# Neighbourhood heads computed two at a time on row and column halves of TensorE

## The chip, the cores and the metric

The kernel runs on one core of a Trainium2 chip. The metric is the device time of one execution, in microseconds. TensorE multiplies, ScalarE (ACT) and VectorE (DVE) do the rest of the arithmetic, and SyncE (SP) issues the loads from HBM.

## What is computed

Two parts follow each other in one program: a two-layer block with a mixture of experts (untouched here), and a two-layer transformer over x (256 tokens) and a context (256 tokens) of width 1024. Its first mixer has 4 differential heads and 8 neighbourhood heads of width 64. The neighbourhood heads, cut to what matters:

```python
# x's queries: keys of x inside a 16-column window of the 64-wide grid, with a bias, and all context keys
s_nb = einsum('bchd,bicjhd->bhcij', q_r, k_r) * scale + bias
s_ctx = einsum('bchd,bnhd->bhcn', q_r, kcx) * scale
p = softmax(concatenate([s_nb, s_ctx], -1))
out_x = einsum(p_nb, v_r) + einsum(p_ctx, vcx)
# the context's queries: plain attention over the context's keys, 8 heads of 64
b_c = plain_attention(heads(bq_c, 8), heads(bk_c, 8), heads(bv_c, 8))
```

The kernel takes x's neighbourhood as a dense 512-wide row of scores (256 context keys, 256 x keys) with a bias matrix of 128 x 256 per head and query block that is -1e30 outside the window.

## The kernel before

**Dense work.** A weight tile is 128x2048 f32 (1 MB). SP loads it to one of 3 RAW places, ScalarE rounds it to its high half WH, VectorE makes the low half WL (3 places of each), and TensorE forms every product as three (L1639 to L1641). With 256 columns a tile is 48 products, in four parts of 12.

**The plan.** `Plan` writes one list of units by hand-made rules and a clock of its own; every engine walks through this same list and takes its units from it. `lin` (L371) adds a weight tile to the list of tiles when its turn comes. Heads are Python generators (`Chain`). After each part of a dense block `weave` (L736) gives every live chain whose time has come one step; `lanes` says how many chains are live, in part 1 two. `yield t` in a chain means: not before t on the plan's clock.

**One head** (`head`, L565): scores `s` (two query blocks, qb 0 and 1), maximum and exponential `e`, normalising `n`, transposes `t`, and after both blocks the values `v`, then a copy of the result. Keys and queries of head hd lie on partitions 0 to 63 when hd is even and 64 to 127 when it is odd, so a score is a product over 64 rows (L1721); values give 64 columns (L1793). With a bias the score is followed by a second product that adds it (L1727). `part=0` are the context's queries, 256 keys; `part=1` those of x, 512 keys.

**Pairs** (`twins`, L639): the same for two heads, until now used by the last mixer's windowed heads (L1345). `s2` (L1732) puts both scores (L1741) and then both masks or biases (L1754 there); `v2` (L1757) takes the heads' values in turns (L1769), one in columns 0 to 63 and one in 64 to 127. It already has a branch for near heads with bias, which no caller used.

**The bias loads.** The bias of head hd lies in one of two places (slot 10 + hd % 2: BIAS and PQ). `head` adds the load when head hd-2 is scored and the chain is live:

```python
while hd > 1 and f"n1.{hd - 2}" not in self.scored:
    yield self.clock + 0.5
t = self.add_tile(("bias", hd), ..., slot=10 + hd % 2, ...)
t.end = ("s", name, 1, 0)
self.put("loads", ("bias", hd))
```

SP issues all tiles, weights and biases alike, in the order of the list (`upto`, L2980, `load`, L2968). Before a load it waits for the end of the tile that had the place before: for a weight tile its split on VectorE, for a bias the scores of qb 1 of the head that used it. `splits_ahead` (L788) keeps a tile's split on ScalarE and VectorE behind the unit for which a load before it in the list must wait.

**Around the change.** `near(0)` and `near(1)` put the context's heads between the dense stages of the mixer's projections; `p.until` ends this with four or five lanes. Then come, with two lanes, the differential heads d1.0 to d1.3 and the near heads n1.0 to n1.7 of x, woven into the context's output projection and its gated layer (`g0c`).

Of the kernel before, what the change touches and what calls it, by code (L numbers as in the profile page):

```python
# [302 lines left out]
class Plan:  # L303


    def __init__(self, io, mem, v):
        self.io = io
        self.units, self.tiles, self.tile, self.stage = [], [], {}, {}
        self.region, self.phase, self.by_split = [], 0, {}
        self.banks, self.tmp, self.pp, self.pt = Rotation(), Rotation(), Rotation(), Rotation()  # L310
        self.heads, self.norms, self.ropes = {}, {}, {}
        self.side, self.live, self.lanes, self.clock = [], [], 2, 0.0
        self.busy, self.at, self.freed_at, self.split_at, self.taken = {A: 0.0, V: 0.0}, {}, {}, {}, {}
        self.n = {"split": 0, "small": 0}
        self.bgc, self.fgc, self.ppc, self.ptc, self.tmpc, self.tmpg = BG, FG, TMP4, TMP4, TMP4, TMP4
        self.ready, self.scored = set(), set()
        self.small = {}
        self.ada = [(l, q) for l in range(2) for q in range(12)]
        self.group, self.grouped = {}, []
        self.asked, self.unturned, self.copied, self.fill_at, self.late = [], [], None, 0.0, []  # L320
        first_order(self)
        second_order(self)
        place_tiles(self.tiles, mem, v)
        place_tiles(self.other[0], mem, v)
        self.units = splits_ahead(self.units, self.tiles, self.tile)
        self.region = splits_ahead(self.region, self.other[0], self.other[1])
# [312 lines left out]
    def twins(self, a, b, nk, bias=False, late=False, **spec):  # L639

        for name, hd in ((a, spec["hd"]), (b, spec["hd"] + 1)):
            self.heads[name] = dict(spec, nk=nk, qbs=2, members=1, bias=bias, sub=False, hd=hd)
        u, near, pair = 0.43 * nk / 256, spec["kind"] == "near", (a, b)

        def room(rotation, choices):
            return sum(x not in rotation.held for x in choices) > 1

        def chain():
            if near and bias:
                hd = spec["hd"]  # L650
                while hd and f"n1.{hd - 1}" not in self.scored:
                    yield self.clock + 0.5
                for x in (hd, hd + 1):
                    t = self.add_tile(("bias", x), self.io["bias"][x], 1, 512, split=False, slot=10 + x % 2,
                                      after=() if hd else [("ps", "v", f"d0.{i}") for i in range(4)] + [("ps", "v", f"n0.{i}") for i in range(8)] + [("band_r",)])
                    t.end = ("s", f"n1.{x}", 1, 0)
                    self.put("loads", ("bias", x))
            blocks, turned = head_needs(self.heads[b])
            blocks, turned = head_needs(self.heads[a])[0] + blocks, head_needs(self.heads[a])[1] + turned
            ready = max([self.at.get(k, 0.0) for k in blocks] + [self.at.get(("roped", r), 0.0) for r in turned])  # L660
            yield ready
            copied = 0.0
            for qb in range(2):
                if qb == 0 and not late:
                    while not room(self.pt, self.ptc):
                        yield self.clock + 0.3
                    for x in pair:
                        self.pt.take(("pt", x), self.ptc, True)
                while len(self.banks.held) > 5:
                    yield self.clock + 0.3  # L670
                free = max([self.bank(("s", x, qb, 0), self.bgc, True) for x in pair])
                at = self.put("s2", a, b, qb, cost=1.25 * u + (0.25 + 0.4 * near) * 2 * bias, after=free)
                if qb:
                    self.scored.update(pair)
                yield at
                while not room(self.pp, self.ppc):
                    yield self.clock + 0.3
                exped, scaled = {}, {}
                for x in pair:
                    self.pp.take(("pp", x, qb), self.ppc, True)  # L680
                    self.small[x, qb, 0] = 4 * (self.n["small"] % 32)
                    self.n["small"] += 1
                    exped[x] = self.freed_at["s", x, qb, 0] = self.put("e", x, qb, 0, after=at)
                    self.banks.let(("s", x, qb, 0))
                yield exped[a]
                for x in pair:
                    scaled[x] = self.put("n", x, qb, 0, after=exped[x])
                yield scaled[a]
                if qb == 0 and late:
                    while not room(self.pt, self.ptc):  # L690
                        yield self.clock + 0.3
                    for x in pair:
                        self.pt.take(("pt", x), self.ptc, True)
                for x in pair:
                    free = self.bank(("t", x, qb), self.bgc)
                    copied = self.freed_at["t", x, qb] = self.put("t", x, qb, cost=u / 2, after=max(free, scaled[x]))
                    self.pp.let(("pp", x, qb))
                yield self.clock
            yield copied
            free = self.bank(("v", a), self.bgc)  # L700
            copied = self.freed_at["v", a] = self.put("v2", a, b, cost=2 * u, after=max(free, copied))
            for x in pair:
                self.pt.let(("pt", x))
                self.at["head", x] = copied
                self.ready.add(x)
        self.side.append(Chain(chain()))

    def rope(self, name, **spec):
# [474 lines left out]
def second_order(p):  # L1183
# [44 lines left out]
    wab0 = Stage("wab0", "rows", "res", io["w_out_ab"], 8, 0, D, "HP", norm="ab0", gate=(0, 0, 1))  # L1228

    def near(t):  # L1230
        for hd in range(4 * t, 4 * t + 4):
            p.head(f"n0.{hd}", 256, kind="near", part=0, hd=hd)

    def diff(t):
        for i in (2 * t, 2 * t + 1):
# [2 lines left out]
    def ropes(g, t):  # L1238
        for blk in (2 * t, 2 * t + 1):
            p.rope(f"{g.name}{blk}", buf=g.more["dst"], blk=blk, n0=T, stage=g.name)  # L1240
    p.lanes = 4
    near(0)
    for t in range(2):
        for g in (aq, ak, av):
# [5 lines left out]
    for g in (bq, bk, bv):  # L1250
        p.lin(g, 1)
        p.turn_one()
    near(1)
    p.begin(wab0, 0)
    p.begin(wab0, 1)
# [7 lines left out]
    p.ppc, p.ptc, p.tmpc = (20, 21), (20, 21), (0, 1)  # L1263
    for i in range(4):
        p.head(f"d1.{i}", 512, members=2, sub=True, kind="diff", part=1, i=i)
    for hd in range(8):
        p.head(f"n1.{hd}", 512, bias=True, kind="near", part=1, hd=hd)
    p.norm("c0.1", src="CTX", tmp="G01", gn=(0, 1, 1), dst="HP", n0=0, of="wab0")
    p.lin_all(wab0, p.follow("c0.1"))
    p.put("gains", 0, 1)  # L1270
# [90 lines left out]
    for j in range(4):  # L1361
        t = p.weight(("wc", j), wc.w, j, 2, 1024)
# [192 lines left out]
def head_needs(spec):  # L1555

    k = spec["kind"]
    if k == "mem":
        return [(f"{n}{spec['l']}", i) for n in ("kvK", "kvV", "q") for i in (6, 7)], []
    if k == "diff":  # L1560
        t = spec["i"] // 2
        need = [("aq", 2 * t), ("aq", 2 * t + 1), ("ak", 2 * t), ("ak", 2 * t + 1)] + [("av", 4 * t + i) for i in range(4)]
        return need, [f"{n}{i}" for n in ("aq", "ak") for i in range(4)] if spec["part"] else []
    if k == "near":
        t = spec["hd"] // 4
        return [("bq", 2 * t), ("bq", 2 * t + 1), ("bk", 2 * t), ("bk", 2 * t + 1)] + [("bv", 4 * t + i) for i in range(4)], []
    hd = spec["hd"]
    return [("ck", 2), ("ck", 3), ("cv", 2), ("cv", 3)], [f"cq{hd // 2}", f"ck{hd // 4}"]
# [1652 lines left out]
```

How the kernel before makes its waits and increments, by code:

```python
    def wait_ge(self, what, *key):  # L90
        what = self.pre + what
        if self.counting:
            return
        n = self.ledger.value[(what,) + key]
        if self.seen.get(what, 0) < n:
            self.eng.wait_ge(self.ledger.sem(what), n)
            self.seen[what] = n
# [5 lines left out]
    def freed(self, key):  # L103
        if key is None or self.counting:
            return
        by = self.ledger.handed.get((self.pre,) + key)
        if by is not None:
            return self.wait_for(by)
        for what in ("free_a", "free_d"):
            if (self.pre + what,) + key in self.ledger.value:
                return self.wait_ge(what, *key)
        raise KeyError(key)
# [1 line left out]
    def wait_for(self, thing):  # L115
        n = self.ledger.value[thing]
        if self.seen.get(thing[0], 0) < n:
            self.eng.wait_ge(self.ledger.sem(thing[0]), n)
            self.seen[thing[0]] = n
# [1 line left out]
    def turn(self, made):  # L121
        made.then_inc(*self.done("turn_" + self.tag, self.steps))
        self.wait_ge("turn_" + self.tag, self.steps)
        self.steps += 1
# [1469 lines left out]
    def weight(key):  # L1595
        t = plan.tile[key]
        pe.wait_ge("w_hi", t.s)
        pe.wait_ge("w_lo", t.s)
        return t
# [1 line left out]
    def consts():  # L1601
        pe.wait_ge("par")
        pe.wait_ge("cst")
# [1 line left out]
    def lin(name, t, i, part, parts, side=None):  # L1605
# [27 lines left out]
        for j, (lh, ll, rh, rl) in enumerate(pairs):  # L1633
            if norm:
                pe.wait_ge("lo", norm, ks[j] // 2)
            if "each" in g.more:
```

## Time and profile before

| | |
|---|---|
| median of 3 runs | 3349.06 us (3346.85 to 3357.35) |
| profiled execution | 3353.13 us, span 3351.3 us |
| TensorE busy | 3197.1 us, 95% |
| VectorE, ScalarE busy | 2331.1 us (70%), 1828.2 us (55%) |
| mean granted TensorE clock | 0.977 |
| HBM | 718.87 MB read, 215 GB/s over the span |

All times in the trace are microseconds from the start of the span. Ends of products on TensorE are modelled, so starts are compared with starts. A product in full f32 leaves two records, which is why one score shows as x2.

### The profile page before, as it was taken

What the parts mean: (1) busy time and instruction counts of PE and PEld (TensorE: products, weight loads), DVE (VectorE), ACT (ScalarE), POOL (GpSimd) and SP (SyncE); (2) the same over time, 40 slices, a digit from 0 to 9 for tenths busy, and PEclk for the clock granted to TensorE, in tenths of its full rate; (3) what the DMA queues carried; (4) which work ended last, traced back from release to release, by engine and by line L of the source; (5) the groups of instructions that cost most, each with busy time, mean ns of one, the idle gap of its engine ahead of it and who ended that gap; (6) DMA issues with size and microseconds to landing.
All of it is one profiled execution on the core that took longest, in us unless ns stands there. A gap on an engine that the chain in (4) does not pass through costs nothing.

```text
span 3351.3 us, 56010 instructions
## 1 busy us (share of the span) xinstructions
PE 3197.1 (95%) x24147; PEld 2976.5 (89%) x24147; DVE 2331.1 (70%) x2984; ACT 1828.2 (55%) x2180; POOL 0.2 (0%) x4
## 2 busy tenths in 40 slices
PE   8999999999999899999999999989899999998898
PEld 7998999999889799999999999878777889985798
DVE  6877655577876588888888888755575556466555
ACT  5564544455545477777777777643464445335443
POOL 0000000000000000000000000000000000000000
PEclk9999999999999899999999999999899999998899
DMA  6433565454335699899899999632223466530353
GB/s 256 167 131 134 178 237 201 152 194 172 115 133 181 239 380 357 334 359 357 336 356 358 338 354 356 249 132 75 102 95 129 157 236 239 214 144 33 151 187 116
DMA packets 102812, 723.62 MB, mean 216 GB/s; under 512 B 11424, under 2 KB 13344, under 8 KB 16672
## 3 DMA queue, kind: packets, MB, share of 16 engines
q1 hardware_dynamic: 102560, 719.97, 58.0%
q8 instruction: 194, 3.18, 0.4%
q14 instruction: 58, 0.48, 0.0%
HBM read 718.87 MB, written 1.05 MB: 215 GB/s over the span
## 4 chain that ended last, share of the span: by engine, by line
PE 78%; DVE 11%; ACT 7%; issue 2%; DMA 1%; SPq 0%; DVEq 0%; ACTq 0%
PE PS L1639 14%; PE PS L1640 14%; PE PS L1641 14%; PE PS L1590 6%; PE PS L1592 6%; PE PS L1591 6%; DVE WL L2424 4%; ACT WH L2015 3%; PE PS L1951 3%; PE PS L1952 3%; PE PS L1953 3%; PE PS L1793 1%; PE PS L1694 1%; PE PS L1721 1%; PE PS L1937 1%
## 5 line engine op out<-in xcount | busy, mean ns | idle before, releaser
L2424 DVE TENSOR_TENSOR WL<-RAW,WH 128x2048 fp32r<-128x2048 f32 (+2 forms) x428 | 962.6, 2252 | 542.1 <-ACT WH L2015 538.7
L2015 ACT ACTIVATE WH<-RAW 128x2048 fp32r<-128x2048 f32 (+2 forms) x428 | 803.5, 1880 | 243.1 <-PE PS L1641 183.0
L1639 PE MATMUL PS<-PH,WH 128*128 128x256 f32 x2464 | 703.7, 286 | 22.5 <-ACT F L2097 6.1
L1640 PE MATMUL PS<-PL,WH 128*128 128x256 f32 x2464 | 694.9, 282 | 0.0
L1641 PE MATMUL PS<-PH,WL 128*128 128x256 f32 x2464 | 694.9, 282 | 0.0
L2424 DVE TENSOR_TENSOR WL<-F,WH 128x2048 fp32r<-128x2048 f32 x210 | 480.6, 2289 | 79.9 <-ACT WH L2015 79.2
L1639 PE MATMUL PS<-HPH,WH 128*128 128x256 f32 (+1 forms) x1648 | 493.9, 300 | 17.6 <-ACT WH L2015 8.7
L1639 PEld LDWEIGHTS PS<-PH,WH 128*128 128x128 f32 x2464 | 467.1, 190 | 29.2 <-issue 20.5
L1640 PE MATMUL PS<-HPL,WH 128*128 128x256 f32 (+1 forms) x1648 | 481.6, 292 | 0.0
L1641 PE MATMUL PS<-HPH,WL 128*128 128x256 f32 (+1 forms) x1648 | 481.3, 292 | 0.0
L1640 PEld LDWEIGHTS PS<-PL,WH 128*128 128x128 f32 x2464 | 467.3, 190 | 0.6
L1641 PEld LDWEIGHTS PS<-PH,WL 128*128 128x128 f32 x2464 | 467.1, 190 | 0.0
L2015 ACT ACTIVATE WH<-F 128x2048 fp32r<-128x2048 f32 x210 | 403.6, 1922 | 72.1 <-PE PS L1953 48.3
L1590 PE MATMUL PS<-WH,PH 128*128 128x256 f32 x1456 | 415.8, 286 | 2.0 <-DVE WL L2424 1.1
L1591 PE MATMUL PS<-WL,PH 128*128 128x256 f32 x1456 | 406.0, 279 | 0.0
L1592 PE MATMUL PS<-WH,PL 128*128 128x256 f32 x1344 | 375.5, 279 | 0.0
L1639 PEld LDWEIGHTS PS<-HPH,WH 128*128 128x128 f32 x1648 | 318.2, 193 | 35.9 <-issue 19.8
L1640 PEld LDWEIGHTS PS<-HPL,WH 128*128 128x128 f32 x1648 | 318.6, 193 | 4.3
L1641 PEld LDWEIGHTS PS<-HPH,WL 128*128 128x128 f32 x1648 | 318.1, 193 | 4.5
L1590 PEld LDWEIGHTS PS<-WH,PH 128*128 128x128 f32 x1456 | 273.8, 188 | 5.3 <-ACT WH L2015 1.3
L1591 PEld LDWEIGHTS PS<-WL,PH 128*128 128x128 f32 x1456 | 274.1, 188 | 2.9
L1592 PEld LDWEIGHTS PS<-WH,PL 128*128 128x128 f32 x1344 | 252.5, 188 | 0.0
(397 smaller groups left out, 4925.3 us busy)
## 6 DMA issues: line engine op xcount, KB each, us to landing
F<-in_moe_w SPq DMA_DIRECT2D x210, 1024.0 KB, 5.3
RAW<-in_ffn_w SPq DMA_DIRECT2D x130, 1024.0 KB, 5.0
RAW<-in_moe_w SPq DMA_DIRECT2D x126, 1024.0 KB, 5.1
RAW<-in_w_in SPq DMA_DIRECT2D x64, 1024.0 KB, 4.9
F<-in_ada_w SPq DMA_DIRECT2D x18, 1024.0 KB, 11.3
RAW<-in_w_kv SPq DMA_DIRECT2D x16, 1024.0 KB, 4.9
G<-in_ada_w SPq DMA_DIRECT2D x15, 1024.0 KB, 9.1
RAW<-in_w_in_ab SPq DMA_DIRECT2D x12, 1024.0 KB, 5.7
```

The source lines that it names most:

```text
L1590: T_.matmul(out, lh, rh, start=i == 0, stop=False)
L1591: T_.matmul(out, lh, rl, start=False, stop=False)
L1592: last = T_.matmul(out, ll, rh, start=False, stop=i == n - 1)
L1639: T_.matmul(out, lh, rh, start=first, stop=False)
L1640: T_.matmul(out, lh, rl, start=False, stop=False)
L1641: last = T_.matmul(out, ll, rh, start=False, stop=end)
L1694: last = T_.matmul(PS[g:g + 32, b, 256 * j:256 * j + 256], own, t.raw[:, k, :], start=at == 0 and j == 0 and k % 2 == 0, stop=at == n - 1 ...
L1951: T_.matmul(out, oh[:, c], wh, start=j == 0 and k == 0, stop=False)
L1952: T_.matmul(out, oh[:, c], wl, start=False, stop=False)
L1953: last = T_.matmul(out, ol[:, c], wh, start=False, stop=j == 13 and k == 1)
L2015: S.activation(mem["WH"][:, t.s % NHL, 0:m], v.raws[t.slot][:, 0:m], ACT.Copy).then_inc(*ac.done("w_hi", t.s))
L2424: V.tensor_tensor(mem["WL"][:, t.s % NHL, 0:m], v.raws[t.slot][:, 0:m], mem["WH"][:, t.s % NHL, 0:m].bitcast(F32), sub).then_inc(*dv.done( ...
```

## The change

All eight context heads and all eight heads of x go through `twins` in place of `head`. In `twins`, with a bias, the pair (hd, hd+1) waits until head hd-1 is scored, adds both bias loads, and now lets 9 us pass on the plan's clock before it goes on to its scores.

```diff
@@ twins, chain() @@
                                       after=() if hd else [("ps", "v", f"d0.{i}") for i in range(4)] + [("ps", "v", f"n0.{i}") for i in range(8)] + [("band_r",)])
                     t.end = ("s", f"n1.{x}", 1, 0)
                     self.put("loads", ("bias", x))
+                yield self.clock + 9.0
             blocks, turned = head_needs(self.heads[b])
@@ second_order @@
     def near(t):
-        for hd in range(4 * t, 4 * t + 4):
-            p.head(f"n0.{hd}", 256, kind="near", part=0, hd=hd)
+        for hd in (4 * t, 4 * t + 2):
+            p.twins(f"n0.{hd}", f"n0.{hd + 1}", 256, kind="near", part=0, hd=hd)
@@
-    for hd in range(8):
-        p.head(f"n1.{hd}", 512, bias=True, kind="near", part=1, hd=hd)
+    for hd in range(0, 8, 2):
+        p.twins(f"n1.{hd}", f"n1.{hd + 1}", 512, bias=True, kind="near", part=1, hd=hd)
```

`twins` was there before. The lines of it that matter:

```python
while hd and f"n1.{hd - 1}" not in self.scored:
    yield self.clock + 0.5
for x in (hd, hd + 1):
    t = self.add_tile(("bias", x), ..., slot=10 + x % 2, ...)
    ...
for qb in range(2):
    ...
    at = self.put("s2", a, b, qb, cost=1.25 * u + (0.25 + 0.4 * near) * 2 * bias, after=free)
    if qb:
        self.scored.update(pair)
```

## Rows read from the trace of the kernel before

**Rows 1.** The page: busy time of TensorE; the chain that ended last, by engine.
```profile
PE 3197.1 (95%) x24147; PEld 2976.5 (89%) x24147; DVE 2331.1 (70%) x2984; ACT 1828.2 (55%) x2180; POOL 0.2 (0%) x4
...
PE 78%; DVE 11%; ACT 7%; issue 2%; DMA 1%; SPq 0%; DVEq 0%; ACTq 0%
```
**Rows 2.** Stretches: length, busy time by engine (instructions), granted clock, DMA share, GB/s.
```profile
2240.00:2360.00 120.00, 119.85 (x657) 98.00 (x658) 63.95 (x162) 45.19 (x95) 0.00 (x0) 1.00 0.21 75
2360.00:2400.00 40.00, 30.99 (x204) 21.79 (x204) 16.39 (x57) 14.49 (x42) 0.00 (x0) 0.74 0.34 132
...
2502.70:2646.60 143.90, 138.97 (x939) 115.11 (x937) 76.11 (x126) 61.31 (x92) 0.00 (x0) 1.00 0.37 136
2646.60:2680.00 33.40, 33.40 (x283) 33.40 (x283) 18.39 (x21) 14.66 (x16) 0.00 (x0) 1.00 0.39 136
```
**Rows 3.** Waits, 2500 to 2650: total us, times, longest.
```profile
PE PS L1781 <- DVE PQ L2665: 3.0, 4, 1.3
```
**Rows 4.** The chain that ended last, around one bias load and around another.
```profile
2516.19 0.64 PE PS L1727 x2
2516.85 0.33 SPq L2978
2517.22 5.03 DMA RAW<-in_ffn_w
2522.33 1.93 ACT WH L2015
2524.28 2.29 DVE WL L2424
2526.68 0.50 DVE PQ L2665
...
2530.78 1.87 PE PS L1793 x8
...
2560.87 8.12 DMA RAW<-in_ffn_w
```
**Rows 5.** Timeline of TensorE around one score of x.
```profile
2502.55 0.28 PE L1641 MATMUL PS<-HPH,WL 128*128 128x256 f32 x1
2502.76 1.12 PE L1721 MATMUL PS<-G 64*128 64x512 f32 x2
2503.81 0.70 PE L1727 MATMUL PS<-BIAS,BAND 128*128 128x256 f32 x2
2504.16 0.47 PE L1639 MATMUL PS<-HPH,WH 128*128 128x256 f32 x1
2504.47 0.28 PE L1640 MATMUL PS<-HPL,WH 128*128 128x256 f32 x1
```
**Rows 6.** Timeline of TensorE, windowed heads in pairs, values and scores.
```profile
3030.05 1.95 PE L1769 MATMUL PS<-G,PQ 128*64 128x256 f32 x16
3035.24 1.13 PE L1741 MATMUL PS<-G 64*128 64x512 f32 x4
3036.30 0.44 PE L1754 MATMUL PS<-BAND 128*128 128x128 f32 x2
```
**Rows 7.** Timeline of TensorE, values of the context's near heads.
```profile
2257.69 2.00 PE L1793 MATMUL PS<-PQ,G 128*64 128x256 f32 x16
...
2389.77 1.97 PE L1793 MATMUL PS<-PQ,G 128*64 128x256 f32 x4
```
**Rows 8.** Waits of SP's queue, 2440 to 2660: total us, times, longest.
```profile
SPq L2978 <- PE PS L1727: 84.5, 6, 23.8
```
**Rows 9.** Stretches without products and right behind them; columns as in rows 2.
```profile
2230.10:2234.50 4.40, 0.03 (x2) 0.03 (x1) 2.82 (x3) 4.34 (x3) 0.00 (x0) 0.86 0.00 0
2234.50:2240.10 5.60, 5.60 (x14) 4.02 (x16) 4.30 (x2) 1.18 (x1) 0.00 (x0) 0.50 0.80 287
...
3156.50:3160.80 4.30, 0.03 (x1) 0.00 (x0) 2.89 (x5) 4.30 (x4) 0.00 (x0) 0.71 0.00 0
3160.80:3165.10 4.30, 4.22 (x20) 4.25 (x21) 4.30 (x2) 1.25 (x1) 0.00 (x0) 0.50 0.73 269
```

## The prediction

> **What bounds the kernel now.** I read the page first: TensorE is busy 95% of the span and holds 78% of the chain that ended last [rows 1], so a microsecond taken from TensorE is worth one, wherever nothing else ends last. Then the stretches by time [rows 2]. The context half of the neighbourhood heads (part 0) lies in 2240 to 2400: to 2360 TensorE is busy 119.85 of 120 us, in the tail from 2360 to 2400 only 30.99 of 40, with the granted clock at 0.74. The x half (part 1) lies in 2502.7 to 2646.6, woven into the context's gated layer, TensorE busy 138.97 of 143.9 us at full clock. After it dense work runs alone: 283 products in 33.4 us, 0.118 us each. A tile has 48 of them, so 5.7 us, in four parts of 12 (1.42 us), and only after a part can another chain put its step. So part 1 is bound by TensorE, with 4.9 us of gaps; its largest waits are for a probability row that VectorE had not finished [rows 3]. Last I read the chain through 2516 to 2531 [rows 4], which decides this case.
>
> **Scores in pairs, part 1.** A single score takes from the dense product at 2502.55 to the second one after it at 2504.47, 1.92 us, less two dense pitches (0.24): 1.68 us, of which 1.05 us is the 64-row product, 0.35 us the bias product, 0.28 us getting in and out [rows 5]. The trace of before has the paired form for the windowed heads at full clock: two products of 64x512 (x4 records) take 1.06 us to the next line at 3036.30, as long as one alone [rows 6]. The mask behind them there is 128 wide and in another type, while a near head has two bias products of 256; I take each at the single's 0.35 us. A pair then costs 1.06 + 0.70 + 0.28 = 2.04 us against 3.36 us. Four pairs times two query blocks: 8 x 1.32 = **-10.5 us**.
>
> **Values in pairs, part 1.** One head's values take 1.87 us (x8 records) [rows 4], and a pair's 1.95 us with 16 records [rows 6]; with the way in and out (0.2) each pair saves 2.05 us, four pairs **-8.2 us**. The transposes are as many as before; put two and two they lose some ways in and out, between 0 and 8 x 0.25 = 2 us; I take 0. One ScalarE copy of the result replaces two, on an engine that is busy less than half of this stretch [rows 2]: nothing.
>
> **Part 0.** The four heads of a group are already put back to back there, and neighbours overlap without any pairing: 16 value records (four heads of 4) in 2.00 us at 2257.69 [rows 7], where one after the other they would need 16/8 x 1.87 = 3.7 us [rows 4]. So the first group gains nothing. In the tail one head's values stand alone at half clock, 1.97 us for 4 records [rows 7], and would overlap with its partner's: **-2 us**. This tail has 9 us of idle from latencies and loads that may fall otherwise, so I bound it by -5 and +4.
>
> **The bias loads and the 9 us: what is queued behind.** This is the step I think decides. SP issues all loads in the order in which the plan adds them, and each waits on SP for its place to come free. A bias load waits for the scores of the heads that had its buffer; every weight tile added later stands behind it. Already now SP sits 84.5 us in six such waits, the longest 23.8 us [rows 8]. It costs little, because a single head n1.h loads its bias when it comes live, which is when head h-2 has finished, long after h-2's last score released the buffer, so the tiles held behind it are wanted only later; TensorE pays in small change, when a late split on VectorE stands before a probability row (the chain's rows at 2524.28 and 2526.68, [rows 4]). In the changed kernel two pairs are live at a time (two lanes). The second has been waiting since it came live for the first one's scores, and adds its two bias loads **in the very weave that puts those scores**, so between the weight tile then being multiplied (T) and the next (T+1). T+1 cannot be issued before the last bias product of the pair's second block ends, and TensorE wants it when T is done. The 9 us of dense work lie behind the loads; they start with exactly the tile that is held.
>
> The price is on the chain: after the score's end at 2516.83 SP issues the bias (2516.85), the tile 0.37 us later, 5.03 us of DMA, 1.93 us of high half on ScalarE, 2.29 us of low half on VectorE, ready at 2526.57: 9.74 us [rows 4]. With a second bias load, 0.4 us, of which most is hidden as the first head's buffer is free 0.35 us sooner: 9.9 us. The dense part of T left after the scores is 0, 1.4, 2.8 or 4.3 us, as the pair's scores fall after its 4th, 3rd, 2nd or 1st part. Following the chains and the plan's clock (9 us are seven parts, one more for the blocks' readiness, five to six parts between a pair's first and second block) I get the 2nd, the 1st, and the 1st or 2nd part for the three handovers (the first pair's buffers are free long before). Stalls of 7.1, 5.6 and 6.4 us, **+19 us**. If all fell after a first part it were 3 x 5.6 = 17; after a fourth, 3 x 9.9 = 30.
>
> **TensorE's clock behind such a stall.** After 4.4 us without products (2230.1 to 2234.5) the granted clock was 0.50 for 5.6 us more, after 4.3 us at 3156.5 it was 0.50 for 4.3 us [rows 9]: 1.2 GHz in place of 2.4, so 2.8 and 2.15 us lost. Part 1 shows 1.00 throughout [rows 2]. Three stalls: 3 x 2.3 = **+7 us** (bounds 5 and 9). The gaps of 4.9 us in part 1 I leave as they are: after a stall three tiles are split in a row on ScalarE and VectorE, ahead of a pair's own normalising, which is the wait of [rows 3] again; up to 2 us more at each handover, in the upper bound only.
>
> **A rule of the skill on this step.** The chain's row at 2516.85 shows the load leaving when the score ends and the tile right behind it. The Trainium skill, Perfetto Trace Analysis, section on the HWDGE DMA instruction, says that the DMA engines on trn2 do not wait on semaphores although they could. By that rule the wait is the issuing sequencer's and holds all that follows, and the trace agrees (84.5 us in six waits); did each transfer wait by itself, tiles would pass the bias, the stalls would be nil and the sum -21 us.
>
> **A rule that speaks against the change.** In part 1 VectorE is busy 76.1 and ScalarE 61.3 of 143.9 us [rows 2]. The Trainium skill, TensorEngine Tiling (Array Packing), section PSUM Bottleneck, warns that tiling speeds up TensorE but not the emptying of PSUM, which may become the bound. Both engines are little more than half busy here, so by the rows the rule takes nothing; would it hold fully, the -18.7 us of part 1 were nil.
>
> **The sum**, against the profiled execution's 3353.1 us (span 3351.3, 1.8 us around it): -10.5 - 8.2 - 2 + 19 + 7 = +5.3 us. The hand count of the parts is my weakest step and the even spread over the four parts would give 3 x 7.8 = 23 us in place of 19, so I lean 1 us up: +6, so 3359 us for a profiled run. The median of the three runs is 3349.1, 4 us below the profiled one; the prediction is for the median, 3355 us.
>
> **Rivals.**
> - *The forecast*: full gain from the halves, nearly given back at three handovers; +1 to +14, about 3350 to 3363. Chance 0.50.
> - *The tiles are in time*: something puts the held tile ahead (the second pair comes live late, or TensorE has other work in the stall), and only the gain is left: -18.7 - 2 = -21 us, 3328 us; with the transposes and some gaps, -26. For it: part 1 as it stands lives with six such waits at a cost of few us. Against it: their slack came from the late loading, which the pairs give up. Chance 0.23.
> - *The handovers cost more (slower side)*: scores end late in their tile, 9.9 us each, clock 2.8 us each, 1.5 us each for the normalising behind three splits: 3 x 14.2 = 43 us - 21 = +22 us, 3371 us. It decides from an average stall of 8.3 us on (3 x (8.3 + 2.3) - 21 = +11). For it: T+1, T+2 and T+3 are loaded together then, and a second tile took 8.12 us to land [rows 4]. Chance 0.22.
> - *Halves don't overlap in a pair with the bias*, or the evacuation binds: -2 + 26 = +24 us, 3373 us. Against it [rows 6]. Chance 0.05.
>
> **How the numbers follow.** What a measurement of this kernel can tell from no change is about 0.3%, 10 us. Faster by more: the second case, 0.23. Slower by more: third and fourth and a fifth of the first, 0.27 + 0.09 = 0.36. The same: 0.41. The range goes from inside the second case (its gain not quite whole) to the third's value: 3329 to 3371 us. The forecast's own range is 3350 to 3363.
>
> **What would show it.** Scores: x4 records of 64x512 in about 1.1 us eight times, followed by two bias products; values x16 in 1.95 us, four times. The handovers: SP waits in fewer waits, each followed at once by two bias loads and up to three weight tiles; TensorE idle 5 to 10 us three times between 2500 and 2600, released by VectorE's low half, at the first product of a tile; granted clock below 1 behind each. Heads of part 1 done near 2610 in place of 2646. Wrong it would be if no wait of TensorE on VectorE's split is longer than 2 us there, or if the second pair's bias loads lie a tile or more behind the first pair's scores.

## The result and the profile after

| | before | after |
|---|---|---|
| median of 4 runs each | 3349.97 us | 3368.72 us (3367.24 to 3373.16) |
| ratio, 95% interval | | 1.0056 [1.0044, 1.0069] |
| profiled execution | 3353.13 us | 3367.24 us, span 3365.5 us |
| TensorE busy | 3197.1 us | 3176.4 us |
| mean granted TensorE clock | 0.977 | 0.975 |

The changed kernel is 18.7 us slower by the medians, 14.1 us by the two profiled executions. TensorE is busy 20.7 us less and still ends later. Where that went is read in the same order as before; in after every line number is one higher.

The stretch of after with x's heads, columns as in [rows 2].
```profile
2502.00:2640.00 138.00, 103.20 (x748) 91.86 (x746) 62.47 (x105) 50.96 (x75) 0.00 (x0) 0.88 0.32 119
```
Against [rows 2] TensorE is busy 103.20 of 138 us where it was 138.97 of 143.9, and the clock is 0.88 in place of 1.00. Nearly all of it is in three waits. TensorE's waits in 2500 to 2640 and SP's in 2440 to 2680 (total us, times, longest):
```profile
PE PS L1640 <- issue: 33.3, 3, 12.4
PE PS L1782 <- DVE PQ L2666: 0.9, 1, 0.9
...
SPq L2979 <- PE PS L1752: 108.8, 3, 36.5
```
L1640 is a tile's first dense product. The profile names nobody ("issue") for its wait; the times in the next rows show what it waited for. SP now stands in three waits of up to 36.5 us on a pair's bias products (L1752), where it stood in six of up to 23.8 us [rows 8]. The first of the three handovers (a pair scored, the next pair's biases loaded) on TensorE, SP, ScalarE and VectorE, from the four timelines of after:
```profile
2521.47 1.13 PE L1742 MATMUL PS<-G 64*128 64x512 f32 x4
2522.53 0.70 PE L1752 MATMUL PS<-BIAS,BAND 128*128 128x256 f32 x2
2523.07 0.59 PE L1752 MATMUL PS<-PQ,BAND 128*128 128x256 f32 x2
2536.02 0.55 PE L1640 MATMUL PS<-HPH,WH 128*128 128x256 f32 x1 [12.35 <-issue]
...
2523.26 0.33 SPq L2979 DMA_DIRECT2D BIAS<-in_bias  x1
2523.70 0.37 SPq L2979 DMA_DIRECT2D PQ<-in_bias  x1
2524.11 1.38 SPq L2979 DMA_DIRECT2D RAW<-in_ffn_w  x3
...
2531.68 1.91 ACT L2016 ACTIVATE WH<-RAW 128x2048 fp32r<-128x2048 f32 x1 [10.93 <-DMA RAW<-in_ffn_w]
...
2533.62 2.29 DVE L2425 TENSOR_TENSOR WL<-RAW,WH 128x2048 fp32r<-128x2048 f32 x1 [11.55 <-ACT WH L2016]
...
2540.83 0.68 DVE L2649 TENSOR_REDUCE SM<-PS 128x1 f32<-128x512 f32 x1
```
In order: the pair's last score ends at 2523.7; SP has issued the first bias load, whose place came free a little sooner, and now issues the second, and at 2524.11 the three weight tiles that stood behind them; the first has landed when ScalarE starts on it at 2531.68; VectorE has its low half at 2535.91; at 2536.02 the dense product starts. In between ScalarE stands still for 10.93 us and VectorE for 11.55. Not all work was missing: the maximum (SM) of the scores that ended at 2523.7 could have run, but VectorE takes its units in the order of the list and came to it at 2540.83, behind the splits of three tiles. By the same order the second handover costs 9.9 us (2565.0 to 2574.9) and the third 11.1 us (2601.8 to 2612.9). The chain that ended last runs through each (at the first through the third tile's landing and split, and from there through this maximum); here the second:
```profile
2561.08 1.07 PE PS L1752 x4
...
2562.17 0.37 SPq L2979
...
2562.59 7.91 DMA RAW<-in_ffn_w
...
2570.52 1.92 ACT WH L2016
2572.44 2.42 issue
2574.86 0.55 PE PS L1640
```
The 2.42 us of "issue" are VectorE's low half (2.29 us) and the signal behind it. Beside [rows 4], where the tile behind a single bias took 5.03 us from its issue to its landing, it took 7.91 us here.

Granted clock behind the first stall (columns as in [rows 2]): half, 1.2 GHz, for 4.98 us of products, then full again.
```profile
2527.30:2541.00 13.70, 4.98 (x23) 5.01 (x24) 6.97 (x4) 5.74 (x3) 0.00 (x0) 0.50 0.55 211
2541.00:2543.60 2.60, 1.74 (x15) 1.54 (x14) 2.46 (x9) 1.55 (x4) 0.00 (x0) 1.00 0.00 0
```
And the gain that was meant is there. A pair's scores and a pair's values, TensorE's timeline of after:
```profile
2512.39 0.28 PE L1642 MATMUL PS<-HPH,WL 128*128 128x256 f32 x1
2512.60 1.13 PE L1742 MATMUL PS<-G 64*128 64x512 f32 x4
2513.66 0.70 PE L1752 MATMUL PS<-BIAS,BAND 128*128 128x256 f32 x2
2514.20 0.59 PE L1752 MATMUL PS<-PQ,BAND 128*128 128x256 f32 x2
2514.44 0.47 PE L1640 MATMUL PS<-HPH,WH 128*128 128x256 f32 x1
2514.74 0.28 PE L1641 MATMUL PS<-HPL,WH 128*128 128x256 f32 x1
...
2547.39 0.27 PE L1642 MATMUL PS<-HPH,WL 128*128 128x256 f32 x1
2547.59 1.95 PE L1770 MATMUL PS<-PQ,G 128*64 128x256 f32 x16
2549.47 0.39 PE L1640 MATMUL PS<-HPH,WH 128*128 128x256 f32 x1
2549.70 0.28 PE L1641 MATMUL PS<-HPL,WH 128*128 128x256 f32 x1
```
Two heads' scores with both biases take 2514.74 - 2512.39 less two dense pitches (0.24) = 2.11 us, two heads' values 2.07 us.

**The balance.** The output's store is issued at 3346.48 before and at 3360.59 after, +14.1 us. I take it apart at two marks, the start of the context's gated layer and its end (the wait for a norm at 2705.9 before and 2722.8 after):

- Up to the gated layer's start: -1.8 us (2446.35 to 2444.58).
- The gated layer, with all heads n1 in it: 259.6 us before, 278.2 after, +18.6. Stalls cost 33.3 us; products at half clock behind them ran 5.0, 3.7 and 3.1 us, so half of that, 5.9 us, is lost; a further half-clock stretch at 2472.7, not there before, costs 1.7 us; the other gaps of part 1 fell from 4.9 to 1.5 us. So 33.3 + 5.9 + 1.7 - 3.4 - G = 18.6, and the pairs gained G = 18.9 us, which three handovers used up.
- From there to the store: 640.6 us before, 637.8 after, -2.8. The change has no unit there. The clock can account for it: the granted clock was half for 44.8 us of it after and for 51.7 us before. One group of the same values' products took 3.05 us from first to last start at 3055.4 before, and 1.57 us at 3071.8 after.

### The profile page after: what moved, and what is told of

It is laid out like the page before. It is cut to its first block, busy times and chain, and to the rows that moved or that the text cites. A ratio compares the mean times of both kernels' runs of the same rounds, so it can differ in the third digit from the quotient of the medians.

```text
span 3365.5 us, 56003 instructions
## 1 busy us (share of the span) xinstructions
PE 3176.4 (94%) x24147; PEld 2968.9 (88%) x24147; DVE 2332.8 (69%) x2984; ACT 1825.8 (54%) x2172; POOL 0.2 (0%) x4
## 3 DMA queue, kind: packets, MB, share of 16 engines
HBM read 718.87 MB, written 1.05 MB: 214 GB/s over the span
## 4 chain that ended last, share of the span: by engine, by line
PE 78%; DVE 11%; ACT 6%; DMA 2%; issue 2%; SPq 0%; DVEq 0%; ACTq 0%
PE PS L1640 14%; PE PS L1641 14%; PE PS L1642 14%; PE PS L1591 6%; PE PS L1593 6%; PE PS L1592 6%; DVE WL L2425 4%; PE PS L1952 3%; PE PS L1953 3%; PE PS L1954 3%; ACT WH L2016 3%; PE PS L1695 1%; PE PS L1770 1%; DMA RAW<-in_ffn_w 1%; PE PS L1794 1%
## 5 line engine op out<-in xcount | busy, mean ns | idle before, releaser
L1640 PE MATMUL PS<-PH,WH 128*128 128x256 f32 x2464 | 704.3, 286 | 23.2 <-ACT F L2098 6.1
L1640 PE MATMUL PS<-HPH,WH 128*128 128x256 f32 (+1 forms) x1648 | 493.9, 300 | 50.5 <-issue 33.7
L1640 PEld LDWEIGHTS PS<-PH,WH 128*128 128x128 f32 x2464 | 467.5, 190 | 30.0 <-issue 21.5
L1640 PEld LDWEIGHTS PS<-HPH,WH 128*128 128x128 f32 x1648 | 319.6, 194 | 69.3 <-issue 52.1
```

The source lines that it names most:

```text
L1640: T_.matmul(out, lh, rh, start=first, stop=False)
```

## The experiments

The theory: SP's wait for the bias buffers holds the next weight tile, and everything else of the change is a gain. Rivals: the 9 us gap does the harm, the pairs gain nothing, part 0 gains or loses. Beside the median, a second measure that leaves out most of the program is the **stretch** from the wait ahead of the mixer's first dense product to the wait for a norm at the gated layer's end: 2230.1 to 2705.9 before = 475.8 us, 2231.6 to 2722.8 after = 491.2 us. It comes from the one profiled execution of each kernel. Edits are against the changed kernel where nothing else is said.

### Part 0 alone

```diff
-    for hd in range(0, 8, 2):
-        p.twins(f"n1.{hd}", f"n1.{hd + 1}", 512, bias=True, kind="near", part=1, hd=hd)
+    for hd in range(8):
+        p.head(f"n1.{hd}", 512, bias=True, kind="near", part=1, hd=hd)
```


> Pairs for the context's heads only; x's heads single as before. Theory Q (weight tiles held behind the bias loads in SP's order cost all that was lost, the pairs themselves gain): no bias in this part, so nothing of the three stalls; the tail's values overlap: 1 to 3 us faster than before, no idle of TensorE over 2 us in 2500 to 2640. Theory P (pairs cost by themselves, through later steps or mode changes): as slow as before or slower by 1 to 4 us.

Measured: 0.9999 [0.9990, 1.0009], 3352.06 us against 3350.86 us; stretch 475.4 us. Pairing the context's heads moves the median by nothing that can be told from noise (the interval is 3 us to either side), so all of the loss is in part 1. The traces show a small gain. From the mixer's first mark to the start of the gated layer the two kernels with single context heads take 216.2 us (before) and 214.4 us (the run "Four places, single heads"), the eleven with pairs 212.0 to 213.8 us, in one execution each: some 2 us.

### The gap ahead of the bias loads

```diff
+                if hd:
+                    yield self.clock + 9.0
                 for x in (hd, hd + 1):
...
-                yield self.clock + 9.0
+                yield self.clock + 3.5
```


> The changed kernel with the 9 us of dense work put between the previous pair's scores and the bias loads, and 3.5 us behind the loads. Theory Q: the tile that stands behind the bias loads is then wanted 9 us or more after the scores released them, so of 33.3 us of idle at the handovers at most 6 are left, no clock loss: 15 to 23 us faster than before, 3327 to 3335 us. Theory G (the 9 us themselves are the cost, wherever they lie, since pairs come late and steps pile up): no better than the changed kernel, 3365 to 3370 us.

Measured: 0.9973 [0.9964, 0.9983], 3341.73 us, 9 us faster than before and 27 us faster than the changed kernel; stretch 461.1 us. The same loads and the same pairs: what differs is where the loads, and the scores after them, stand in the list, so that is what cost the time. It gained less than I expected (9 us against 15 to 23). TensorE's waits in 2500 to 2660, and the chain through the largest:
```profile
PE PS L1772 <- ACT PQ L2166: 6.7, 3, 5.1
...
2521.73 9.22 DMA RAW<-in_ffn_w
...
2531.03 1.91 ACT WH L2018
2532.94 0.98 ACT PQ L2166 x2
...
2534.06 1.97 PE PS L1772 x8
```
TensorE no longer waits for a tile. It waits for a pair's own transposed rows (ACT PQ), which stand on ScalarE behind the split of the tile that landed late. The hold is still there, in another queue.

### No gap

```diff
-                yield self.clock + 9.0
```


> The changed kernel without the 9 us. Theory Q: the tile is held just the same until 12.3 us after the scores; the next pair's first scores (2 us) move into the stall, and TensorE waits there for the bias to land instead: three stalls stay, 24 to 32 us in sum, time 0 to 8 us below the changed kernel, 3360 to 3369. Theory G: without the gap no stall, 3325 to 3335 us.

Measured: 1.0035 [1.0021, 1.0049], 3362.89 us; stretch 486.3 us; the three waits of the first dense product are 9.5, 11.5 and 10.3 us, together 31.3. The gap is neither the cause nor a cure: without it the same three stalls stand in the same place, at a dense tile's first product. I had expected TensorE to wait for the bias of the next pair instead; no such wait is in the trace.

### The weight tiles two ahead in the list

Weight tiles of the gated layer are added to the list up to two tiles before their turn, so that they stand ahead of the bias loads:
```diff
+            for t_ in range(t, min(t + 3, g.ncols // 256)) if g.name.startswith("g0cc") else ():
+                if (g.name, t_) not in self.tile:
+                    self.begin(g, t_)
```
and likewise in the order of the gated layer's first part.

> The changed kernel with the weight tiles of the context's gated layer entered in the list two tiles before their use, so that two tiles stand ahead of the bias loads; heads, gap and everything on TensorE as in the changed kernel. Theory Q: the first held tile is wanted two tiles (11.4 us and the heads' steps) after the scores' tile, so the stalls fall from 33.3 us to under 3 and the clock stays at 1: 19 to 24 us faster than before, 3325 to 3331 us. Theory G or P: unchanged, about 3368 us.

Measured: 0.9999 [0.9989, 1.0009], 3349.55 us; stretch 470.4 us. That is 19 us faster than the changed kernel and no better than before; I had expected 19 to 24 us below before. Waits of TensorE (2500 to 2660) and the chain:
```profile
PE PS L1791 <- DVE PQ L2675: 13.7, 3, 10.6
...
2523.73 7.35 DMA RAW<-in_ffn_w
...
2531.16 1.92 ACT WH L2025
...
2533.10 2.29 DVE WL L2434
2535.39 0.61 DVE SM L2658
```
The tile that TensorE needs is in time, but the one behind the bias loads still lands late, and its split, issued in the order of the list, stands on VectorE ahead of the very pair's maximum (SM) and probabilities (PQ): 10.6 us of waiting. Three engines walk the same list, so moving a tile within it moved the hold from the dense product to the normalising.

### Four places for the biases

The bias of head x goes to one of four places, two of them free memory, so that no bias load waits for the pair just scored, only for the one before that. The list is that of the changed kernel, the gap too.
```diff
-    slot=10 + x % 2, after=() if hd else [...]
+    slot=(10, 11, 20, 21)[x % 4], after=() if hd > 2 else [("sub_y", "d1.2"), ("sub_y", "d1.3")] if hd else [...]
...
+     v.raws += [mem["TMP2"][:, 0, :], mem["TMP2"][:, 1, :]]
```


> The changed kernel with four places for biases in place of two (the second and fourth pair's lie in two scratch buffers that the differential heads have left): the list of tiles, its order, the transfers and TensorE's order are those of the changed kernel, only the bias loads no longer wait for the scores of the pair just before. Theory Q (the wait in SP's order is the cause): no idle at the handovers beyond 2 us each, clock 1.00 in 2500 to 2640, 15 to 22 us faster than before, 3329 to 3336 us. Theory D (bias loads and weight tiles crowd each other in the DMA queues, wherever the wait is): first tile behind the biases still lands 7 us or more after issue, stalls of 3 us or more each, no faster than before.

Measured: 0.9943 [0.9925, 0.9961], 3332.66 us against 3352.11 us; stretch 457.9 us, 33.3 us below after. The stretch and SP's waits:
```profile
2502.00:2640.00 138.00, 132.16 (x1018) 119.57 (x1017) 79.75 (x131) 64.88 (x91) 0.00 (x0) 0.99 0.44 155
...
SPq L2980 <- PE PS L1753: 42.7, 2, 22.3
SPq L96 <- DVE G L2685: 17.8, 1, 17.8
```
SP still stands 42.7 us in two waits for a pair's bias products, and TensorE loses nothing by them: the third pair's load waits for the first pair's scores and is issued at 2529.72, long before the second pair's last scores at 2551.32, behind which it stands in the list. The first two loads to the new places wait too, for a differential head's norm (17.8 us). One 4.4 us wait of TensorE is left from it, by the mechanism of the experiment before this one (a split on VectorE ahead of a probability row). This is the experiment that decides: with no load waiting for the pair just scored, and nothing else of the list changed, the kernel is 19.5 us faster than before.

### Bias loads only when the pair before is finished

```diff
-                while hd and f"n1.{hd - 1}" not in self.scored:
+                while hd and f"n1.{hd - 1}" not in self.ready:
...
-                yield self.clock + 9.0
+                yield self.clock + 3.5
```


> Two places, but a pair's bias loads are listed when the previous pair has finished its values, as single heads had it, then 3.5 us of dense work. Theory Q: the scores released the places a tile or more before, the held tiles are back in time; idle in part 1 under 6 us, 15 to 20 us faster than before. Better than the kernel with the gap before the loads (3341.7 us) by up to 6 us, since its 5.1 us wait for a transposed row behind a late split goes too. Theory D: as that kernel or worse.

Measured: 0.9958 [0.9941, 0.9974], 3337.99 us with two places only; stretch 464.2 us. The profiled execution, 3345.67 us, was the slowest of the four, so its span isn't compared and its stretch says little. I had expected 15 to 20 us below before, and got 14: a 6.1 us wait of TensorE is left behind a late split on ScalarE, as in the second experiment, where I had expected it to go.

### Values head after head

Four places, and in `v2` the two loops swapped, so the second head's products come after the first's instead of in turns:
```diff
-        for k in range(n):
-            for o, ls, pt in terms:
+        for o, ls, pt in terms:
+            for k in range(n):
```


> As e6_four_places, but a pair's values are put head after head (k 0 to 3 of the one, then of the other) and not in turns. If only turns make the column halves overlap: 8 records more in sequence for each of 4 pairs of x and 3 of 8 windowed, 1.7 us each, and 0.9 us for the context's: 20 us slower than e6. If TensorE overlaps what stands back to back, as the context's single heads did before: within 3 us of e6.

Measured: 0.9968 [0.9955, 0.9980], 3340.91 us; span 3343.3 us against 3331.8 us for four places alone. One pair of x in four places alone, then here:
```profile
2538.96 1.95 PE L1771 MATMUL PS<-PQ,G 128*64 128x256 f32 x16
2540.84 0.39 PE L1641 MATMUL PS<-HPH,WH 128*128 128x256 f32 x1
```
```profile
2538.60 2.86 PE L1771 MATMUL PS<-PQ,G 128*64 128x256 f32 x16
2541.39 0.39 PE L1641 MATMUL PS<-HPH,WH 128*128 128x256 f32 x1
```
From the first value to the next dense product 1.88 us in turns and 2.79 us head after head. One head alone takes 1.87 us [rows 4], so two without overlap would take 3.74 us. In sequence they overlap in part: by the single records the second head's first product starts 0.92 us after the first head's, beside the first's second half. So neither of my two cases (20 us slower, or within 3 us) came about. Twelve pairs run these loops on 512 keys (four of x, eight of the last mixer), 12 x 0.91 = 10.9 us; the span of the profiled executions grew by 11.5, the median by 8.3. The context's pairs, 256 keys, took the same either way (0.70 and 0.71 us between first and last start).

### Scores head after head

Four places, and each head's score followed by its own bias, so that no two scores lie side by side:

```diff
+            elif spec["kind"] == "near":
+                ...
+                last = T_.matmul(out[name][:, 256:512], mem["BAND"][:, 0:128].bitcast(F32), tile.raw[:, 0, qb * T:qb * T + T], start=False, stop=True)
```


> As e6_four_places, but x's near pairs put score, bias, score, bias, so that the two 64-row products don't stand side by side. Prices the row halves alone: my sum has 8 x 1.06 = 8.5 us; 7 to 10 us slower than e6. If the row halves did not overlap in a pair: no difference.

Measured: 0.9975 [0.9966, 0.9985], 3343.71 us, 11 us above four places alone; stretch 465.3 us, 7.4 us longer, while TensorE waits 2.1 us less in it (2.9 for 5.0 us on a probability row). One block of a pair:
```profile
2538.98 1.12 PE L1743 MATMUL PS<-G 64*128 64x512 f32 x2
2540.03 0.70 PE L1750 MATMUL PS<-TMP,BAND 128*128 128x256 f32 x2
2540.66 1.12 PE L1743 MATMUL PS<-G 64*128 64x512 f32 x2
2541.71 0.70 PE L1750 MATMUL PS<-TMP,BAND 128*128 128x256 f32 x2
2542.06 0.47 PE L1641 MATMUL PS<-HPH,WH 128*128 128x256 f32 x1
```
From the first score to the next dense product 3.08 us, where a pair side by side takes 1.84 us (2512.60 to 2514.44 in after): 8 x 1.24 = 9.9 us, the price of the lost overlap.

### Neither wait nor hold

The edits of two sections above together: four places, and bias loads when the pair before is finished, with the gap of 3.5 us.

> Four places for biases and the loads listed when the previous pair has finished its values, 3.5 us of dense work behind them. Theory Q: no load in 2500 to 2660 waits for something less than a tile old, so even the 4.4 us that e6 kept (its first such load waited 17.8 us for a differential head's norm, and a late split stood before a probability row) goes or shrinks under 2 us: 19 to 25 us faster than before, the best so far, 3326 to 3333 us. If e6's rest has another cause: as e6, 19 us.

Measured: 0.9946 [0.9932, 0.9959], 3332.23 us against 3351.22 us; stretch 453.5 us. The stretch in part 1, TensorE's waits and SP's:
```profile
2502.00:2640.00 138.00, 134.43 (x1046) 121.45 (x1045) 82.28 (x132) 64.97 (x92) 0.00 (x0) 1.00 0.44 157
...
PE PS L1641 <- DVE HPL L2600: 2.7, 2, 1.8
...
SPq L96 <- DVE G L2685: 12.5, 1, 12.5
```
No load waits for scores any more, and no wait of TensorE is above 1.8 us. The stretch is 4.4 us shorter than with four places alone; the medians (3332.23 and 3332.66) don't tell the two apart. Both beat the kernel before by 19 us.

### Four places, single heads

The kernel before, with `slot=(10, 11, 20, 21)[hd % 4]` in `head`, no pairs.

> The kernel before (single heads) with the four places. Splits what the places give from what the pairs give. Theory Q with pairs gaining 18 to 21 us by themselves: the single heads lose only their 4.9 us of gaps in part 1, 0 to 4 us faster than before. If the places are most of e6's gain: 10 us or more faster.

Measured: 0.9989 [0.9980, 0.9998], 3348.18 us; stretch 470.5 us. The places alone bring 1 to 7 us by the interval, 3.7 us by the ratio. So of the 19 us of four places with pairs, about 15 belong to the pairs. The stretches of the two kernels in which no load waits for scores (this one, and the last one with pairs) differ by 17.0 us.

### One bias per pair

Both heads of a pair read the even head's bias; the loads of the odd heads are left out (so their scores have the wrong bias). Two bias loads ahead of the held tiles become one.
```diff
-                for x in (hd, hd + 1):
+                for x in (hd,):
...
+                    self.tile["bias", x + 1] = t
```


> The changed kernel, but a pair loads one bias and both heads use it (left out: the bias of the odd heads, so the result differs). The wait in SP's order is as before; in front of the held tiles stands one transfer of 256 KB, not two. If two bias loads delay the first held tile (theory B): it lands 5.1 us after its issue in place of 7.5, the stalls shrink from 33.3 to 25 to 27 us, 7 to 9 us faster than the changed kernel. If it is the three tiles issued at once (theory C): it lands at 7.5 us as before, only SP's 0.4 us per handover goes, 1 to 2 us faster than the changed kernel.

Measured: 1.0031 [1.0021, 1.0042], 3361.21 us, 7.5 us faster than after; stretch 483.2 us. TensorE's wait and the chain at the second handover:
```profile
PE PS L1641 <- issue: 25.6, 3, 9.8
...
2559.02 0.33 SPq L2980
...
2559.39 5.43 DMA RAW<-in_ffn_w
```
The held tile takes 5.43 us to land behind one bias load (5.07 us at the third handover) against 7.91 and 7.67 us behind two, with three tiles issued at once either way. The stalls are 7.7 us shorter in all. So the second bias load is the difference between the 5.03 us that I had read from [rows 4] and what the handovers cost.

## Why the prediction was right and where it was not

The time, 3368.7 us, lies in the range (3329 to 3371) but outside the forecast's own range (3350 to 3363), and the slower side at 0.36 was given less than "the same" at 0.41. The mechanism and every direction were right. What came about is nearest to the third case, "the handovers cost more": its condition, an average stall above 8.3 us, was met with 11.1. That its time, 3371 us, is so close is partly luck: the stalls were longer than its 9.9 us (11.1), the clock cost 2.0 us a stall and not 2.8, and its 1.5 us of late normalising did not show, misses that nearly cancel.

**Scores in pairs, -10.5: held.** 2.11 us a pair and block against 2.04 forecast, so 8 x (3.36 - 2.11) = 10.0 us. Taking the overlap away cost 9.9 us.

**Values in pairs, -8.2: held.** 2.07 us a pair, so 4 x 2.07 = 8.3 us saved. By the balance the pairs of x saved 18.9 us where I had 18.7, and scores and values make 18.3 of it. The transposes gave nothing, as forecast: from the last dense product before them to the second after, a pair's take 1.11 to 1.31 us, one head's 0.68; less two dense pitches each, 0.87 to 1.07 us against 2 x 0.44.

**Part 0, -2: the traces agree, the median can't tell.** The gated layer starts 1.8 us earlier although the mixer started 1.5 us later; against the trace of before the way there is 3.3 us shorter, against the other kernel with single heads 1.4 us.

**Bias loads and held tiles, +19: right in kind, 14 us too small.** This is the term that failed, and it failed in two of its inputs.

- *The tile's landing.* I took 9.9 us from the end of the score to the dense product, with 5.03 us for the landing behind one bias load, and charged the second bias load its 0.4 us of issuing, mostly hidden. It delays the tile's landing: 7.5 (2524.11 to 2531.6), 7.91 and 7.67 us. The whole way is 12.3, 12.7 and 12.5 us, 7.8 us more in all. Shown by the run with one bias per pair. The row of 8.12 us in [rows 4] would not have given this price: it belongs to the second tile of a burst behind one bias, not to the first tile behind two.
- *The part of the tile after which the scores fell.* I had the 2nd, the 1st, and the 1st or 2nd, 10.6 us of dense work left in all. The stalls say otherwise: 12.4, 9.9 and 11.1 us are the whole way less 0, 2.8 and 1.4 us, the 4th, 2nd and 3rd part: 4.2 us in all, 6.4 us less. I had called it my weakest step and allowed 1 us for it; the even spread, 3 x 7.8 = 23, would have been the better value; with the 7.8 us of the landing it gives 31, against 33.3 measured.

**A rule of the skill, once more.** SP's row at 2524.11, three weight tiles issued at once right behind the bias loads, again agrees with what the Trainium skill says in Perfetto Trace Analysis, section on the HWDGE DMA instruction: the wait is the issuing sequencer's, not the transfer's. SP stood 108.8 us in three waits, with loads behind them that have nothing to do with the biases. By that section the profiler's slice of such an instruction begins when its semaphores are satisfied, so the wait isn't in it; in this trace it is in SP's waits and in the chain, while the stalled product on TensorE has no name for its releaser.

**A rule that spoke against the change.** The emptying of PSUM, which the Trainium skill warns of in TensorEngine Tiling (Array Packing), section PSUM Bottleneck, did not bind: with neither wait nor hold VectorE is busy 82.28 and ScalarE 64.97 of 138 us, and no wait of TensorE there is above 1.8 us.

**The clock, +7: held.** 5.9 us behind the three stalls, 1.7 us in a stretch elsewhere.

**Gaps left at 4.9 us: they fell to 1.5 us.** A likely reason, not tested: while TensorE is stalled, the pairs' normalising catches up. With neither wait nor hold, where TensorE doesn't stall, they are 3.6 us. My bound of 2 us more at each handover had the wrong sign; the one place where normalising stood behind three splits, at the first handover, cost TensorE 0.9 us. The same mechanism, a late split in front of a head's own rows, was real, though: it came out once the tile's wait was gone, as 5.1 us, 10.6 us and 6.1 us in the three kernels that only moved loads or tiles in the list. I had not seen that it caps what moving them can bring.

The difference between forecast sum and profiled result, 14.1 - 5.3 = 8.8 us, is then: stalls +14.3, clock +0.6, pairs -0.2, gaps -3.4, part 0 +0.2, and -2.8 behind the gated layer, where the change has no unit (the rest is rounding).

**The other rivals.** That the tiles are in time didn't come about: at all three handovers they were issued right behind the end of the scores. The size of that case was nearly right all the same: with the hold gone the kernel takes 3332.7 us, where I had 3328 for it. That the halves don't overlap is excluded by the 2.11 and 2.07 us.

**What would show it.** The records came as described, with two exceptions. TensorE's three stalls have no releaser's name, where I had VectorE's low half; that half's row, ending at 2535.91, shows it. And the last pair's values came at 2658.7 and not near 2610: a date that I had given without the stalls in it.

## What to carry to other kernels

In an issuing queue that runs in order, a load's wait for its buffer is a wait of every load behind it, and of every engine that takes its work from the same order. When an edit moves a load to the place where its buffer is just being released, cost the next independent load from that release to its use, with all transfers that are issued ahead of it; then give the waiting load a buffer of its own before you shift it: here shifting won 0 to 14 us and left the wait to another engine, a free buffer won 19. Half-array products side by side are worth having, and most with their instructions in turns: one half after the other kept about half of the gain.

## What the runs showed of the hardware

- Column halves overlap even when one head's products follow the other's, but late: 16 records of value products took 1.88 us to the next dense product in turns, 2.79 us in sequence; without overlap it would be 3.74 us (2 x 1.87).
- Row halves overlap whole: two heads' scores take 1.06 us to the next line, as one head's 1.05 us; with a bias product between them they take 3.08 us with both biases in place of 1.84 us.
- Two loads of 256 KB ahead of one of 1 MB delay its landing by about 2.5 us (7.91 and 7.67 us against 5.43 and 5.07 us); one delayed it by little against the 5.0 us median of such tiles. Why the second weighs so much more than the first stays open.
- After stalls of 12.4, 9.9 and 11.1 us TensorE ran the next 5.0, 3.7 and 3.1 us of products at 1.2 GHz.
